# A hybrid decoder step on one core: which queue stores the expert rows, when the rows of an extra pass are fetched, and how its passes are looped

## What is computed

```python
def hier_moe(x, w_group, b_group, w_router, b_router, w_gate_up, w_down):
    ...
    g_idx = jnp.argmax(g_logits, axis=-1)
    ...
    top_v, top_i = lax.top_k(e_in_group, TOP_K_IN_GROUP)
    weights = g_w * jax.nn.softmax(top_v, axis=-1)
    ...
    def expert_block(a):
        xb, e = a
        gate, up = jnp.split(xb @ w_gate_up[e], 2, axis=-1)
        return (jax.nn.silu(gate) * up) @ w_down[e]
    ...
    y = jax.ops.segment_sum(yp[dest] * w_sorted[:, None].astype(x.dtype), tok_sorted, num_segments=n)
    return y.reshape(bn, t, d)
```

## Time and profile before

| | us |
|---|---|
| median of 3 runs (lowest, highest) | 3058.38 (3057.62, 3061.38) |
| the profiled execution | 3057.78 |
| its span | 3056.2 |
| expert stage of layer 0, about | 1090 to 1878 |
| expert stage of layer 1, about | 2303 to 3020 |

### The profile page before, as it was taken

How to read it: one execution, slowest core, us unless ns; L and a number is a source line. 1 busy time by engine, 2 the same in 40 slices (tenths; PEclk the granted TensorE clock), 3 DMA queues, 4 the chain that set the end, 5 groups by cost and what they waited for, 6 DMA issues and landing times. The chain is left out here.

```text
span 3056.2 us, 25007 instructions
## 1 busy us (share of the span) xinstructions
PE 2148.9 (70%) x8185; PEld 991.7 (32%) x8186; DVE 499.4 (16%) x1033; ACT 309.6 (10%) x587; POOL 163.0 (5%) x127
## 2 busy tenths in 40 slices
PE   5989884688878466586668661899946676676572
PEld 1225332366664332222223220455432222222220
DVE  0000873311111400000000002111140000000002
ACT  0020113211110110000000000100010000000000
POOL 0000110000001200000000002000120000000003
PEclk9999996666669678788888785899968897887795
DMA  8970046133420174667688886010036877788783
GB/s 280 328 268 0 4 136 275 30 106 104 142 88 0 68 305 148 257 246 274 262 310 321 321 327 239 2 55 0 29 152 239 337 290 308 270 330 342 284 316 137
DMA packets 198481, 605.70 MB, mean 198 GB/s; under 512 B 18191, under 2 KB 18736, under 8 KB 198281
## 3 DMA queue, kind: packets, MB, share of 16 engines
q1 hardware_dynamic: 172776, 550.53, 47.7%
q10 hardware_dynamic: 13257, 28.46, 2.5%
q0 software_dynamic: 12384, 25.87, 2.5%
HBM read 552.15 MB, written 53.06 MB: 198 GB/s over the span
## 5 line engine op out<-in xcount | busy, mean ns | idle before, releaser
L682 PE MATMUL ps<-ring,W 128*64 128x512 f32 x2400 | 570.1, 629 | 168.2 <-ACT W L805 106.1
L695 PE MATMUL ps<-ring,W 128*64 128x512 f32 x1200 | 354.5, 744 | 55.0 <-DVE W L1430 39.7
L682 PEld LDWEIGHTS ps<-ring,W 128*64 128x64 f32 x2400 | 203.6, 146 | 516.6 <-issue 515.7
L805 ACT ACTIVATE W<-ps 128x512 f32<-128x512 f32 (+8 forms) x258 | 137.3, 548 | 1666.5 <-DMA x_rows<-W 717.9
L695 PEld LDWEIGHTS ps<-ring,W 128*64 128x64 f32 x1200 | 112.5, 170 | 251.6 <-issue 251.6
L1424 DVE TENSOR_TENSOR W<-W,ps 128x256 f32<-128x256 f32 x64 | 27.0, 421 | 971.9 <-ACT W L1041 971.9
L688 PE MATMUL ps<-C,W 128*128 128x128 f32 x150 | 36.9, 334 | 208.7 <-DVE W L1424 197.6
L450 PE MATMUL ps<-ring,cT 128*9 128x512 f32 x384 | 169.7, 597 | 9.4 <-DMA ring<-in_w_ada_dram 9.0
L782 PE MATMUL ps<-hT,ring 128*128 128x512 f32 x384 | 170.7, 597 | 0.5 <-DVE W L1448 0.5
L631 PE MATMUL ps<-W,ring 128*128 128x4 f32 x512 | 114.4, 355 | 3.4 <-ACT W L805 3.4
L528 PE MATMUL ps<-ring,hT 128*128 128x512 f32 (+1 forms) x240 | 115.1, 639 | 1.9 <-DVE W L1160 1.9
(11 more groups left out here) (269 smaller groups left out, 1559.7 us busy)
## 6 DMA issues: line engine op xcount, KB each, us to landing
ring<-in_w_gate_up_dram SPq DMA_DIRECT2D x128, 2048.0 KB, 18.6
ring<-in_w_down_dram SPq DMA_DIRECT2D x64, 2048.0 KB, 19.4
ring<-in_w_ada_dram SPq DMA_DIRECT2D x24, 2048.0 KB, 12.0
x_rows<-X ACTq DMA_DIRECT2D x1, 18944.0 KB, 52.2
ring<-in_cache_k_dram SPq DMA_DIRECT2D x64, 256.0 KB, 2.9
ring<-in_cache_v_dram SPq DMA_DIRECT2D x64, 256.0 KB, 2.9
W<-x_rows SPq DMA_DIRECT2D x32, 512.0 KB, 16.9
x_rows<-W SPq DMA_DIRECT2D x60, 256.0 KB
```

Of the source, the lines that this page charges most:

```text
L682: x = mm(ps[CAP * z:CAP * z + CAP, 2 + j, :], xt[:, k, :], at[:, :, 256 * z:256 * z + 256], start=(k == 0), stop=(k == KD - 1))
L695: x = mm(ps[CAP * z:CAP * z + CAP, 5 + j, :], ht[:, k % 2, CAP * (k // 2):CAP * (k // 2) + CAP], ring[:, 3 * j + 2, at:at + 512], start=(k ...
L805: return fn(out, src, ACT.Copy, **k)
```

## The change

Result rows, base and extra, are stored from ACT's queue, right behind the instruction that copies them (base) or behind a wait for DVE's copy (extra); SP stores nothing. POOL fetches the rows of the next extra pass as soon as PE's transposes have read those of the pass before; it stores nothing, and DVE waits for the landing of the extra store before. After the stage POOL reads the table for the number of extra stores and waits for them. In `further` the first extra pass stands alone, the second in an If behind it, and the loop, from the third pass on, in an If behind that.

```diff
@@ further
-                with eng.Fori(1, NB) as b:
-                    with eng.If(passes > b):
-                        one_pass(before + b)
+                one_pass(before + 1)
+                with eng.If(passes > 2):
+                    one_pass(before + 2)
+                    with eng.If(passes > 3):
+                        with eng.Fori(3, NB) as b:
+                            with eng.If(passes > b):
+                                one_pass(before + b)
+                            eng.nop()
+                        eng.nop()
                     eng.nop()
                 eng.nop()
@@ SP
-                def rows_out(n, j):
-                    sp.wait_ge(M["y_ok"], done(l, n))
-                    sp.dma_start(y_rows(bass.ds(CAP * n, CAP)), yh[:, j, :]).then_inc(y_out[j], 16)
...
-                    if not (isinstance(n, int) and n == 0):
-                        rows_out(n - 1, 1 - j)
...
-                rows_out(E - 3, 1)
@@ PE and ACT, once at the start
+            pe.sem_inc(F["products"], 4)
+            act.sem_inc(F["stored"], 16)
@@ ACT
                     def one_pass(c):
-                        act.wait_ge(F["products"], c * 4 - 3)
+                        act.wait_ge(F["products"], c * 4 + 1)
                         copy(flat(xT2), ps[:, 0, :]).then_inc(F["act"], 1)
-                        act.wait_ge(F["products"], c * 4 - 2)
+                        act.wait_ge(F["products"], c * 4 + 2)
                         fn(hh2, ps[:, 2 + j, 0:256], ACT.Silu).then_inc(F["act"], 1)
+                        act.wait_ge(F["dve"], c * 3)
+                        carry(act)
+                        act.dma_start(y_rows(bass.ds(c * CAP + (E - 1) * CAP, CAP)), yh2).then_inc(F["stored"], 16)
...
                     copy(yh[:, j, :], ps[:, 5 + j, :]).then_inc(M["y_ok"], 1)
+                    act.wait_ge(M["y_ok"], done(l, n))
+                    carry(act)
+                    act.dma_start(y_rows(bass.ds(CAP * n, CAP)), yh[:, j, :]).then_inc(y_out[j], 16)
...
-                for j in range(2):
-                    n = E - 2 + j
-                    act.wait_ge(M["y_ok"], done(l, n))
-                    act.dma_start(y_rows(slice(CAP * n, CAP * n + CAP)), yh[:, j, :]).then_inc(y_out[j], 16)
@@ DVE
-                        dve.wait_ge(F["products"], c * 4)
+                        dve.wait_ge(F["products"], c * 4 + 4)
+                        dve.wait_ge(F["stored"], c * 16)
+                        carry(dve)
                         v.tensor_copy(yh2, ps[:, 5 + j, :]).then_inc(F["dve"], 1)
@@ POOL
                     def one_pass(c):
-                        at = bass.ds(c * CAP + (E - 1) * CAP, CAP)
-                        pool.dma_start(xg2, x_dram[at, :]).then_inc(F["gathered"], 16)
-                        pool.wait_ge(F["dve"], c * 3)
+                        pool.wait_ge(F["products"], c * 4 - 3)
                         carry(pool)
-                        pool.dma_start(y_rows(at), yh2).then_inc(F["stored"], 16)
-                        pool.wait_ge(F["stored"], c * 16)
-                        carry(pool)
+                        pool.dma_start(xg2, x_dram[bass.ds(c * CAP + (E - 1) * CAP, CAP), :]).then_inc(F["gathered"], 16)
...
+                before = pool.value_load(tab[l][0:1, 1, E - 1:E], min_val=0, max_val=XTRA - 1)
+                passes = pool.value_load(tab[l][0:1, 0, E - 1:E], min_val=1, max_val=NB)
+                pool.wait_ge(F["stored"], (before + passes) * 16)
+                carry(pool)
```

More of the change, by code:

```diff
@@ L1416, in one_pass @@
                         tt(hh2, hh2, ps[:, 2 + j, 256:512], ALU.mult).then_inc(F["dve"], 1)
-                        dve.wait_ge(F["products"], c * 4 - 1)
+                        dve.wait_ge(F["products"], c * 4 + 3)
                         v.tensor_copy(flat(hhT2), ps[:, 4 + 3 * j, 0:256]).then_inc(F["dve"], 1)
-                        dve.wait_ge(F["products"], c * 4)
+                        dve.wait_ge(F["products"], c * 4 + 4)
+                        dve.wait_ge(F["stored"], c * 16)
+                        carry(dve)
                         v.tensor_copy(yh2, ps[:, 5 + j, :]).then_inc(F["dve"], 1)
```

## The result

The changed kernel takes 3093.68 us in the median (3092.52 to 3099.65) where the kernel before, beside it, takes 3058.44: ratio 1.0117, 95% interval 1.01 to 1.0135. It is 1.2% slower. The forecast was 2976 us, and its wider range (8 in 10) ended at 3020. The profiled execution took 3093.38 us, its span is 3091.6. In its profile the lines of the five programs have moved by a few: SP's loads are L347 (before L341), ACT's silu L1045 (L1041); PE's keep their numbers.

What follows compares the result with a forecast made beforehand. The two DMA engines that carry the row stores were taken to bound both expert stages. Idling recovered 75 us plus tails 9 less 2 added made 82 us off 3057.8: 2976 us, range 2950 to 2995, 8 in 10 within 2940 to 3020.

Steps and rivals of the forecast that it cites:

- The pair of engines: Both expert stages: two DMA engines carry the row stores besides their weights, 541 kB a step, and set 20.9 us.
- The store on another queue: Steady step: stores on ACT's queue still load the same two engines, so the step stays at 20.8 us.
- The parts of the sum: Whole kernel: 75 us of idling recovered at extra passes, 9 us at tails, less 2 us added, 82 us off.
- 63 - 5 = 58: Layer 0's extra passes: 63 us of the two engines' idling, of which 5 us stay.
- 5 us of idling were to stay: First double visit of layer 0: the two store-carrying engines still idle some 5 us after the change.
- only the pair's idle time counts: Extra passes: of some 195 us of PE's delay, only the 80 us in which the two store-carrying engines idle count.
- rival 2: Expert loop: PE's longer code no longer stays and is fetched again; 3148 us, slower by 3%, chance 0.06.
- a form that nibbles: Expert loop: a smaller stall for PE's code takes back part of the gain, 2985 to 3000 us, chance 0.17.
- a stall up to that: Expert steps: a code stall within PE's spare 7.9 us costs nothing in steady steps, 5 to 20 us around extra passes.
- the six steps of 20.77 us: Middle of an expert stage: measured steps of 20.77 us an expert, against PE's 12.9 us, leaving PE 7.9 us spare.
- The third rival: Extra passes: they are held about as long as now, only tails are gained, 3040 to 3058 us, chance 0.07.
- The tails: Ends of both stages: one last store is left, 6.7 us instead of 11.92 us for two; 9 us less together.

Runs made afterwards that it cites:

- e11: The kernel before with each base store issued as two DMAs of 64 partitions, nothing else: 2839.18 us, ratio 0.9273.
- e1: The changed kernel with the old loop over the extra passes, one body in each step: 2997.61 us, ratio 0.9784 to the kernel before.
- e3: The changed kernel with only the first extra pass ahead of the loop, 1611 PE instructions: 2989.25 us, ratio 0.9763 to the kernel before.
- e9: The kernel before with only the base stores moved to ACT's queue: 3011.26 us, ratio 0.9833.
- e12: The kernel before with never executed extra-pass bodies on PE, two for three of four experts and one for the fourth: 3127.72 us, ratio 1.0219.
- e7: The changed kernel with one extra pass ahead of the loop and each row store as two DMAs: 2754.27 us, ratio 0.8998 to the kernel before.
- e6: The changed kernel with each row store issued as two DMAs of 64 partitions: 3093.64 us, ratio 1.0093 to the kernel before.

## Why the prediction was wrong

**What bounds the kernel: right, but stretched too far.** The pair of engines bounded the steady step; e11 takes it away and gains 7.3%, 97 us in layer 0's stage and 102 in layer 1's. But "bounds both stages" does not hold step by step, as is told below. The store on another queue did not relieve it: in e1, which has all stores on ACT and no stalls, six steps of layer 1 lie between these two down products

```profile
2706.78 6.46 PE L689 MATMUL ps<-ring,W 128*64 128x512 f32 x16 [3.06 <-DMA ring<-in_w_down_dram]
...
2835.05 5.47 PE L689 MATMUL ps<-ring,W 128*64 128x512 f32 x16 [4.26 <-DMA ring<-in_w_down_dram]
```

21.4 us each, where the kernel before has 20.77: no relief (and 0.6 us more, which was not pursued); PE now waits for the down weights. The rule of the Trainium skill that the prediction weighed (DMA: Bandwidth & Descriptors, Rules for kernel authors), that queues share the engines and the outermost dimension limits how many of them a DMA uses, agrees with both runs.

**The parts of the sum: right in kind, some of them too large.** e1 is the change without its loop form, e3 with half of it: there the seven visits with one pass have lost their empty turns, the two with two passes have not. Down products of e1, as in the first rows above:

```profile
L689 PE MATMUL ps<-ring,W x624: 592/592/1116, 1110.0 to 1806.0; 128*64 128x512 f32 x156
L689 PE MATMUL ps<-ring,W x576: 592/593/1116, 2277.2 to 2948.9; 128*64 128x512 f32 x192
```

Layer 0 is 48 us shorter (forecast 63 - 5 = 58), layer 1 is 7 (17), the stretch between and the end together 10.5 (9 - 2 = 7). In medians e1 gains 2.2%, 66 us, and e3 2.4%, 72 us, where the sum was 82. In layer 1, where all visits have one pass, e3's stage takes 658.3 us, 20 less than before: there the forecast was right once the turns are gone. What was too large is layer 0, 697.9 us in e3, 46 less where 58 were forecast. In its double visits 5 us of idling were to stay; with the turns still in them, e1 has about 12 us with a share of 0.07 in the first (e3 has 0.06):

```profile
1176.00:1188.00 12.00, 5.85 (x20) 1.74 (x18) 0.69 (x1) 0.00 (x0) 0.00 (x0) 0.72 0.07 23
```

The forecast's rule that only the pair's idle time counts did not hold for the parts: e9 alone gained 51 us where that rule gives 15 to 35. So e3's total (72 us, where the sum was 82) comes near the forecast with a split that is not the forecast's, and that is in part luck.

**The step that failed: the code of three bodies, put at nothing in the sum, with rival 2's chance and price.** The sum has no term for it ("Three bodies instead of one: see the second rival"); measured, it is 102 us, from e1 to the changed kernel. The mechanism of rival 2 is the one that happened, in the signs that it named: queue 8 packets in the expert loops, gaps of PE ahead of an expert's first product. Its size of the loop (1824 + 300 = 2124) is 0.5% off the counted 2135. Two things in rival 2 were wrong.

The first is the chance. A loop of 1087 instructions that is not fetched again says nothing of one twice as long; there was no row on the other side, and the estimate already stood above the only figure at hand. The chances given were 0.06 for "slower" and 0.17 for a form that nibbles, where the rows left it open either way. The figure at hand is the Trainium skill's (Advanced Engine Details and Errata, ISA Cache): 128 KB on TensorE, in lines of 256 instructions, which is 2048. Taken as the size of a loop that stays, which is an estimate, e12 with 1988 would still fit. It did not, so the measurement decides: what a loop may have here ends between 1619 and 1988. Why it ends below 2048 no run tells; a line more for where the loop begins in its first line, or one fetched ahead, are guesses.

The second is the price: "a stall up to that costs nothing in the steady steps and takes back 5 to 20 us around the extra passes". The first half held in layer 1 (81.1 us a turn against 83.1), for a stall of 6.9 us an expert against 7.9 to spare, a near thing; in the last eight experts of layer 0 it did not (22.0 us against 20.7). The second half failed. The forecast took the six steps of 20.77 us for the whole stage. Up to 1660 us, three quarters of layer 0's stage, no step between visits is of that kind: the five visits come four experts apart, and behind each the pair is ahead and PE sets the pace at 13 to 15.5 us. There a stall counts in full. The range of 5 to 20 us stands against these 102. Layer 0 is 97 us longer than in e1 (793.4, 696.0), layer 1 only 3 (674.9, 671.7). Moreover a stall is not only its gap, as is told in the last section.

**The third rival** (idling stays) was not it: the extra passes are short after the change. In the first visit with two of them, the wait for gathered rows is gone and the copy follows after 1.3 us (timeline of PE after; the earlier trace rows before):

```profile
1178.83 0.68 PE L717 MATMUL ps<-C,W 64*128 64x64 f32 x8 [1.31 <-DVE W L1425]
1180.67 8.78 PE L682 MATMUL ps<-ring,W 128*64 128x512 f32 x32 [1.16 <-ACT W L805]
...
1196.47 7.09 PE L682 MATMUL ps<-ring,W 128*64 128x512 f32 x32 [1.47 <-DVE W L1425]
```

One sign that the prediction named did not come, though. The pair was to idle only some 5 us in a double visit; in the changed kernel it has 20 us at a share of 0.09 there, nearly as before:

```profile
1176.00:1196.00 20.00, 15.08 (x66) 5.28 (x62) 2.23 (x4) 0.98 (x2) 0.51 (x1) 0.91 0.09 27
```

PE was held by stalls ahead of the visit, and the pair may have got ahead of it by as much; no run tests that.

The tails came out near the forecast: the last store of layer 1 lands 7.78 us after its start, where it took 11.92 behind another, and 6.7 were forecast.

```profile
3047.04 7.78 DMA x_rows<-W
```

## What to carry to other kernels

Before a body is copied in a loop of an engine, count that engine's instructions in the whole loop: this kernel took 0.2% longer with 532 instructions added to PE's 1087, and 2.6% longer with 1024, though none of them ran; the instruction queue of the profile (39 or 47 packets, or 161 and more) told here at a glance on which side a kernel was. A spare time read from the steady steps covers a stall only in these; look for the steps in which the engine sets the pace before you call it hidden. And if a transfer's outermost size leaves it on two of sixteen engines, mend that first: alone it was worth 7.3% here, three times what all the reordering gave.

## What the runs showed of the hardware that was not expected

A loop that doesn't fit is fetched whole. In layer 0 the changed kernel has 52 packets in 574 us, 0.85 MB, and in 82 us of layer 1, about a turn (2717 to 2799), nine:

```profile
q8 instruction: 9, 0.15, 0.7%
```

By the line size of the Trainium skill (Advanced Engine Details and Errata, ISA Cache; 16 KB, 256 instructions) 2135 instructions are 8.3 lines, an estimate by which nine packets a turn would be all of it; the trace agrees, with nine packets of 0.15 MB. The total does too: of the 126 packets more than before, some 16 are the longer code fetched once (twice the eight of e3), and 110 are left for the twelve jumps back of two stages, 9.2 each. e12 with 1988 has nearly as many packets (161) and its longest stall is as long (10.2 us), so little or nothing is kept of a loop slightly too long.

Not every stall is the loop's. The four experts behind the loop run once in each stage, and in layer 1 of the changed kernel three of them still have gaps of 3.3 to 3.6 us where three bodies are jumped over; in e7, where it is two bodies, one of the four has one (3.30 us). Their code is fetched for the first time there.

Nor is the time in bytes, which are 0.7% of the engines' time, but in PE's waiting for them: 3.6 us where a `further` of three bodies is skipped, 10 us at the turn of the loop. In the four gaps of the turn shown above the DMA share is 0.96 to 1.04; what a fetch costs on idle engines stays open.

And a gap costs twice. The products behind it start at a lower granted clock. Windows of the changed kernel, before a gap, behind the gap of 3.61 us, and behind that of 10.05 us (columns as in the earlier trace rows):

```profile
2776.80:2780.30 3.50, 3.50 (x16) 1.18 (x16) 0.00 (x0) 0.00 (x0) 0.00 (x0) 1.00 0.97 362
2784.10:2787.00 2.90, 2.90 (x10) 1.06 (x12) 0.00 (x0) 0.00 (x0) 0.00 (x0) 0.67 1.03 417
...
2809.00:2812.00 3.00, 3.00 (x8) 0.99 (x10) 0.00 (x0) 0.00 (x0) 0.00 (x0) 0.50 0.19 74
2813.00:2817.50 4.50, 4.50 (x22) 1.39 (x18) 0.00 (x0) 0.00 (x0) 0.00 (x0) 1.00 0.51 126
```

The granted clock is 1.00 (2.4 GHz) before. After 10 us in which PE did nothing it is 0.50 (1.2 GHz) over the first 3 us, and then 1.00 again; after 3.6 us of idling the mean of the first 2.9 us is 0.67. Three us at half the clock are worth about 1.5 us, an estimate, and that is most of the 1.7 us by which a gate and up group of 8.8 us exceeds one of 7.07. With four such groups a turn it is a quarter of what the stalls cost (6.9 of 27.5 us in e6's terms).
